# Loads in order of use and residual adds on Pool in a one-layer decoder step

## The reference

```python
h = x + 0.5 * rmsnorm(swiglu(rmsnorm(x, g1pre)), g1post)       # width 2816
b_a, c_a, h_a, u, v = split(rmsnorm(h) @ w_in)                 # 5 x 512 columns
y_a = b_a * causal_dwconv3(c_a * h_a)
y_b = u * (tril(W_s[head]) @ rmsnorm(v) + b_s)                 # chunks of 128 positions
h = h + rmsnorm(concat(rmsnorm(y_a), rmsnorm(y_b)) @ w_out)
h = h + 0.5 * rmsnorm(swiglu(rmsnorm(h)))
h = h + rmsnorm(sigmoid(h @ W_pg) * (p @ W_pp))                # input embedding
```

## Time and profile before

| | us |
|---|---|
| median of three runs | 1377.72 (1377.32 to 1531.78) |
| the profiled execution | 1379.56 |
| its slowest core, first to last instruction (core 7) | 1378.5 |
| its fastest core | 1363.9 |
| TensorE busy on core 7 | 1305.4 |
| Vector, Act, Pool busy | 524.1, 415.0, 94.3 |

### The profile page before, as it was taken

One profiled execution on the slowest core, in us unless ns is written; L12 is line 12 of the kernel. 1 busy time (PEld: TensorE's weight loads), 2 busy tenths in 40 slices (PEclk: granted clock), 3 DMA queues, 4 the chain that ended last, 5 costly groups with the idle time before them and its releaser, 6 DMA issues.

```text
span 1378.5 us, 18493 instructions; the slowest of 8 cores (1363.9 to 1378.5 us)
## 1 busy us (share of the span) xinstructions
PE 1305.4 (95%) x6710; PEld 647.0 (47%) x6710; DVE 524.1 (38%) x691; ACT 415.0 (30%) x860; POOL 94.3 (7%) x185
## 2 busy tenths in 40 slices
PE   5999999999989999999996999999999899999995
PEld 3566664455445666644441444444444344444442
DVE  2322223356677222213365322223466922221337
ACT  3311112344355111111175111123333721111136
POOL 2100000001000200000010000000010020000000
PEclk8999999999999999999997999999999999999998
DMA  9997422129525963231289974321295297423123
GB/s 215 178 222 154 68 47 46 31 45 183 92 42 82 175 124 62 47 69 25 45 202 211 220 159 87 63 53 31 62 175 107 50 147 141 91 48 68 31 39 122
DMA packets 88185, 139.87 MB, mean 101 GB/s; under 512 B 58272, under 2 KB 58528, under 8 KB 87456
## 3 DMA queue, kind: packets, MB, share of 16 engines
q0 software_dynamic: 25296, 90.25, 39.7%
q1 hardware_dynamic: 62800, 48.43, 13.2%
HBM read 206.03 MB, written 9.51 MB: 156 GB/s over the span
## 4 chain that ended last, share of the span: by engine, by line
PE 84%; DVE 6%; DMA 3%; issue 3%; ACT 3%; POOL 0%; DVEq 0%; ACTq 0%; POOLq 0%; SPq 0%
PE ps L218 56%; PE ps L538 23%; PE ps L527 3%; DMA y<-big 2%; DVE zsc L227 2%; DVE nT L227 1%; DVE big L231 1%; DMA h<-xT 1%; ACT big L223 1%; DVE big L227 1%; DMA ring<-w 1%; ACT nT L223 1%; ACT sg L223 1%; ACT L223 1%; DVE nbr L227 1%
## 5 line engine op out<-in xcount | busy, mean ns | idle before, releaser
L218 PE MATMUL ps<-nT,ring 128*128 128x384 bf16 (+1 forms) x4160 | 785.3, 351 | 18.7 <-DVE nT L227 9.2
L218 PEld LDWEIGHTS ps<-nT,ring 128*128 128x128 bf16 x4160 | 409.7, 99 | 392.3 <-issue 44.0
L231 DVE TENSOR_TENSOR big<-ps,sg 128x384 bf16<-128x384 f32 (+1 forms) x220 | 133.9, 610 | 489.4 <-PE ps L218 479.4
L538 PE MATMUL ps<-ring,big 128*128 128x512 bf16 x1320 | 285.5, 379 | 4.5 <-DVE big L231 4.5
L223 ACT ACTIVATE sg<-ps 128x384 f32<-128x384 f32 (+1 forms) x237 | 127.1, 537 | 506.4 <-PE ps L218 496.8
L538 PEld LDWEIGHTS ps<-ring,big 128*128 128x128 bf16 x1320 | 128.9, 98 | 161.0 <-issue 6.2
L259 POOL DMA_DIRECT2D ring<-w x170 | 89.9, 535 | 1104.5 <-PE ps L218 621.6
L223 ACT ACTIVATE big<-ps 128x1024 bf16<-128x1024 f32 (+4 forms) x88 | 75.4, 870 | 229.4 <-PE ps L538 192.4
L227 DVE SCALAR_TENSOR_TENSOR zsc<-ps,st,gains 128x1024 f32<-128x1024 f32 x51 | 65.4, 1282 | 192.5 <-ACT st L223 192.2
L538 PE MATMUL ps<-ring,nT 128*128 128x512 bf16 x480 | 105.4, 379 | 1.0 <-DVE big L231 1.0
L231 DVE TENSOR_TENSOR big<-ps,big 128x384 f32<-128x384 f32 (+3 forms) x77 | 50.8, 686 | 62.1 <-PE ps L218 34.4
(11 more groups left out here) (63 smaller groups left out, 369.3 us busy)
## 6 DMA issues: line engine op xcount, KB each, us to landing
ring<-w POOLq DMA_DIRECT2D x170, 512.0 KB, 14.5
h<-x SPq DMA_DIRECT2D x17, 512.0 KB, 30.7
y<-big SPq DMA_DIRECT2D x13, 512.0 KB, 10.7
gains<-gain SPq DMA_DIRECT2D x12, 512.0 KB, 9.3
h<-xT SPq DMA_DIRECT2D x3, 1536.0 KB, 13.2
big<-xT SPq DMA_DIRECT2D x2, 2048.0 KB, 20.0
y<-zsc SPq DMA_DIRECT2D x4, 512.0 KB, 12.0
big<-pT POOLq DMA_DIRECT2D x2, 512.0 KB, 7.9
```

Of the source, the lines that this page charges most:

```text
L218: ins = nc.tensor.matmul(out_ap, l, r, start=(i == 0), stop=(i == n - 1))
L231: return DVE.mark(nc.vector.tensor_tensor(out=out, in0=in0, in1=in1, op=op))
L538: ins = nc.tensor.matmul(o.t, lhs(k), sv, start=(k == 0), stop=(k == nk - 1))
```

## The change

- Pass 0's tile 1 of x is issued right behind tile 0 and the gain columns; two fills are issued ahead of Pool's last memset, tile 2 of x behind it, then the other fills. Warm-up is 110 matmuls, and 40 more after the statistics of tiles 0 and 1, which now both come ahead of the first stage, as do their applies. Tile 2's squares move to a hook of their own after (1,0), its statistics and apply to the middle of (1,1).
- Pass 1: tile 0 of x is issued by a hook in the down stage when block 8's matmuls are done (the junk output of that stage moves from j0 14 to 0); its squares go to another place in big, over which tile 1's load comes after the statistics. Squares after block 1, statistics after the first group, apply after block 3. Tile 1 of x is issued after the first group; fills at the stage's start are one, and one more after each of two groups. Tile 1's squares and the rest get two hooks.
- Mixer: six square buffers in place of four; `norm_tile` is split, its statistics stay, its apply goes behind the spatial epilogue; group A's statistics go behind U's second projection.
- Output projection and embedding stage: the residual adds are `nc.gpsimd.tensor_tensor` (but for the last block of `ple`). Down stages keep Vector.
- Pass 1, last group of `ple`: the embedding matmuls come ahead of the gate projections, over four pairs.

```diff
...
-    def get_pair():
-        i = rot["pair"] % 3
+    def get_pair(n=3):
+        i = rot["pair"] % n
...
+    def tt_p(wait, out, in0, in1, op):
+        POOL.wait(wait)
+        return POOL.mark(nc.gpsimd.tensor_tensor(out=out, in0=in0, in1=in1, op=op))
...
     xt_load(PASSES[0], 0)
     ev_gc = gc_sem.add(nc.sync.dma_start(out=gc_t[:], in_=gcol_d))
+    xt_load(PASSES[0], 1)
...
+    for _ in range(2):
+        issue_next()
     ev_pc = pchain(nc.gpsimd.memset(carry_t[:], 0.0))
+    xt_load(PASSES[0], 2, [ev_pc])
     while wr["issued"] < NSLOT:
         issue_next()
-    for ti in range(1, 3):
-        xt_load(PASSES[0], ti, [fill_ev[ti - 1][0]])
 
     act([ev_ones], out=st_t[:, 0, 0:1], in_=ones_t[:, 0:1], func=AF.Ln)
-    warm = banks[7]
-    PE.wait(ev_ones)
-    for _ in range(90):
-        ins = nc.tensor.matmul(warm.t[:, 0:128], ones_t[:], ones_t[:], start=True, stop=True)
-    warm.free = PE.mark(ins)
+
+    def warm_up(n):
+        PE.wait(ev_ones, banks[7].free)
+        for _ in range(n):
+            ins = nc.tensor.matmul(banks[7].t[:, 0:128], ones_t[:], ones_t[:], start=True, stop=True)
+        banks[7].free = PE.mark(ins)
+
+    warm_up(110)
...
+    def x_sq_at(P, ti):
+        c0, w = P.tiles[ti]
+        if (P.idx, ti) == (1, 0):
+            return bigf[:, 4096:6144].bitcast(BF16).rearrange("p (k s) -> p k s", k=8)
+        return nT_t[:, :, c0:c0 + w]
...
         for k in range(8):
             PE.wait(sq[k // 2])
-            ins = nc.tensor.matmul(bank.t[:, 0:w], ones_t[:], nT_t[:, k, c0:c0 + w], start=(k == 0), stop=(k == 7))
-        ev = PE.mark(ins)
+            ins = nc.tensor.matmul(bank.t[:, 0:w], ones_t[:], sqt[:, k, :], start=(k == 0), stop=(k == 7))
+        ev = xstat_ev[P.idx, ti] = PE.mark(ins)
...
         e = stt([e3, gain_ev[gi], zfree[zi]], zsc_t[:, zi, :], pt[:], r, gain(gi))
         lo.free = hi.free = e
-        h_ev[b] = zfree[zi] = tt([e], h_t[:, b, :], h_t[:, b, :], zsc_t[:, zi, :], ALU.add)
+        h_ev[b] = zfree[zi] = add([e, h_ev[b]], h_t[:, b, :], h_t[:, b, :], zsc_t[:, zi, :], ALU.add)
...
             last = b == P.nb - 1
             pair, ev = proj_block(P, b, nk, lambda k, b=b: lhs(b, k), 4, fl, wait(b), last)
             if hooks and b in hooks:
-                hooks[b]()
+                hooks[b](ev)
             st = post_stat(b, pair, ev, c, j0)
-            e = post_apply(b, pair, st, gpost)
+            e = post_apply(b, pair, st, gpost, tt if lag == 1 else tt_p)
...
-        sq = [bigf[:, ZR + 2048 + 256 * i:ZR + 2304 + 256 * i].bitcast(BF16) for i in range(4)]
+        sq = [bigf[:, o:o + 256].bitcast(BF16) for o in [ZR + 2048 + 256 * i for i in range(4)] + [ZR + 4096, ZR + 4352]]
...
-        def norm_tile(ti, bank_of=get_bank):
+        def norm_stat(ti, bank_of=get_bank):
+            c0, w = P.tiles[ti]
+            par = ti % 2
+            return rstd_bc(*stat(y_ev[ti][1], w, bank_of), zsc_t[:, par, 512:1024], w, rs_free[par])
...
+        def norm_apply(ti, e_b):
             c0, w = P.tiles[ti]
             par = ti % 2
             ra, rb = zsc_t[:, par, 0:512], zsc_t[:, par, 512:1024]
-            ya, yb, ev_u = y_ev[ti]
-            e_b = rstd_bc(*stat(yb, w, bank_of), rb, w, rs_free[par])
+            ya, _, ev_u = y_ev[ti]
             e = None
             for c in range(8):
...
             if ti >= 1:
-                norm_tile(ti - 1)
+                e_b = norm_stat(ti - 1)
...
-            e_a = rstd_bc(*stat(sqa, w), zsc_t[:, ti % 2, 0:512], w, rs_free[ti % 2])
+            if ti >= 1:
+                norm_apply(ti - 1, e_b)
             sqb = []
             for c in range(4):
                 b, evl = proj(fU, evU, ti, c)
+                if c == 1:
+                    e_a = rstd_bc(*stat(sqa, w), zsc_t[:, ti % 2, 0:512], w, rs_free[ti % 2])
                 y = mixo[:, c, c0:c0 + w]
                 e = tt([evl, mix_e], y, b.t[:, 0:w], y, ALU.mult)
                 b.free = e
@@ -807,8 +832,8 @@
             y_ev[ti] = (e_a, sqb, evl)
         release(fU, evl)
 
-        def tail():
-            norm_tile(nt - 1, get_tp)
+        def tail(ev):
+            norm_apply(nt - 1, norm_stat(nt - 1, get_tp))
...
         if N is not None:
-            xt_load(N, 0, [nT_ev[P.nb - 1]])
-            xt_load(N, 1)
-            pay_owed([nT_ev[P.nb - 1]], NFILL + 3)
+            pay_owed([nT_ev[P.nb - 1]], NFILL + 1)
...
         for gi, grp in enumerate(groups):
             lastg = gi == len(groups) - 1
             sig = {}
+            emb = {}
+            early = N is None and lastg
+            if early:
+                emb = {b: embed(b, b == grp[-1], 4) for b in grp}
             for b in grp:
                 pair, ev = proj_block(P, b, 8, lambda k, b=b: nT_t[:, k, b * 128:(b + 1) * 128], 4, fg, [nT_ev[b]],
-                                      lastg and b == grp[-1])
+                                      lastg and b == grp[-1], 4 if early else 3)
                 gate_ev[b] = ev
-                if N is not None and gi == 2 and b == grp[0]:
-                    xs["st"] = x_stat(N, 0, xs["sq"], get_tp)
                 pt, lo, hi = pair
                 e = act([ev, gb_guard(b)], out=gb(b), in_=pt[:], func=AF.Sigmoid)
                 lo.free = hi.free = e
                 sig[b] = e
+                if N is not None and b == 1:
+                    xs["sq"] = x_square(N, 0)
+                if N is not None and b == 3:
+                    x_apply(N, 0, *xs["st"], [gate_ev[3]])
                 del nT_ev[b]
             zev = {}
             for b in grp:
-                pair = get_pair()
+                pair, ev = emb[b] if early else embed(b, lastg and b == grp[-1])
...
-                xs["sq"] = x_square(N, 0, [gate_ev[3]])
             st = {}
             for b in grp:
                 st[b] = rstd_of(gb(b), sg_t[:].rearrange("p a s -> p (a s)"), [zev[b]], D)
-            if N is not None and gi == 2:
-                xs["ev"] = x_apply(N, 0, *xs["st"])
+            if N is not None and gi == 0:
+                xs["st"] = x_stat(N, 0, xs["sq"], get_tp)
             for b in grp:
                 r, e3 = st[b]
                 e = stt([e3, gain_ev[base + GPLE]], gb(b), gb(b), r, gain(base + GPLE))
                 nxt["stt"] = e
-                e = tt([e], gb(b), gb(b), h_t[:, b, :], ALU.add)
+                e = (tt if b == P.nb - 1 else tt_p)([e], gb(b), gb(b), h_t[:, b, :], ALU.add)
                 SP.wait(e)
                 out_ev[b] = y_sem[b].add(nc.sync.dma_start(out=y_d[P.rows[b]:P.rows[b] + 128, :], in_=gb(b)))
                 if N is not None and b < N.nb:
                     h_free[b] = e
+            if N is not None and not lastg:
+                pay_owed(None, NFILL + 2 + gi)
+                if gi == 0:
+                    xt_load(N, 1, [xstat_ev[1, 0]])
...
-    x_apply(PASSES[0], 0, *x_stat(PASSES[0], 0, x_square(PASSES[0], 0), get_bank))
-
-    def start_mid(ti):
-        def f():
-            x_apply(PASSES[0], ti, *x_stat(PASSES[0], ti, x_square(PASSES[0], ti), get_bank))
-        return f
+    first = x_stat(PASSES[0], 0, x_square(PASSES[0], 0), get_bank)
+    x_apply(PASSES[0], 0, *first)
+    second = x_stat(PASSES[0], 1, x_square(PASSES[0], 1), get_bank)
+    warm_up(40)
+    x_apply(PASSES[0], 1, *second)
...
+    def start_square():
+        nx["sq"] = x_square(PASSES[0], 2)
+
+    def start_mid():
+        x_apply(PASSES[0], 2, *x_stat(PASSES[0], 2, nx["sq"], get_bank))
...
+    def next_square():
+        nx["sq"] = x_square(PASSES[1], 1)
+
     def next_mid():
-        e = x_apply(PASSES[1], 1, *x_stat(PASSES[1], 1, x_square(PASSES[1], 1), get_bank))
+        e = x_apply(PASSES[1], 1, *x_stat(PASSES[1], 1, nx["sq"], get_bank))
         SP.wait(e)
         for b in range(PASSES[1].nb):
             x_load(PASSES[1], b, [h_free[b]])
...
         if P.idx == 0:
-            gu_stage(P, 2, guard1, {(0, 0): (0, start_mid(1)), (1, 0): (1, start_mid(2)), (2, 0): (0, start_loads),
+            gu_stage(P, 2, guard1, {(1, 0): (1, start_square), (1, 1): (0, start_mid), (2, 0): (0, start_loads),
                                     (8, 0): (0, late_consts)},
                      [(0, 0), (0, 1), (1, 0), (1, 1), (0, 2), (1, 2)])
         else:
-            gu_stage(P, 3, guard1, {(0, 0): (1, next_mid)})
+            gu_stage(P, 3, guard1, {(0, 0): (1, next_square), (1, 0): (1, next_mid)})
...
         hold_fills(1)
 
+        def next_x(ev):
+            xt_load(PASSES[1], 0, [ev])
...
         tok_stage(P, NFF, 6, lambda b, k: hmid[:, k, b * 128:(b + 1) * 128], lambda b: [hm["ev"]],
-                  base + G2POST, 4.0, 1, 14, cast)
+                  base + G2POST, 4.0, 1, 0, cast, {8: next_x} if N is not None else None)
...
```

More of the change, by code:

```diff
@@ L463, in build_program @@
     xn_ev = {}
+    xstat_ev = {}
+    def x_sq_at(P, ti):
[3 more added lines that the diff above has]
+        return nT_t[:, :, c0:c0 + w]
     def x_square(P, ti, wait=None):
         c0, w = P.tiles[ti]
+        sqt = x_sq_at(P, ti)
```

(64 more changed lines are left out.)

## The result

The changed kernel takes 1366.04 us in the median, 0.9912 of the kernel before, interval [0.9884, 0.9941]: 12 us gained where 35 were forecast. The profiled execution took 1364.25, its slowest core (core 3) 1363.2, against 1378.5 before.

The account below looks back on a forecast made before the run. TensorE was taken as the bound, with time to win only where it waits or runs at its lower clock. Gains 6 + 11 + 0 + 17 + 1 = 35 us against the median 1377.72 gave 1343, range 1326 to 1365.

Parts of the forecast that it names:

- Start: Start of the first pass: x tile 1 loaded earlier lands at 19, first stage ends at 201.6 against 208.25; 6 us gained.
- Mixer: Mixer tiles: moved statistics and norm save 16.9 us, less 5.8 for new waits; 11 us gained, bounds 7 and 16.
- Output projections: Residual adds moved to Pool in the output projections: 3.6 us per block, no change; bounds 5 gained, 7 lost.
- the formula (4.9 + A)/2 = 3.6: Output projections: time per block of a four-engine loop over two blocks, A being Pool's add, taken as 2.3 us.
- The rival: Pool's add and Vector's two-SBUF-input instructions exclude each other: output projections lose 10.5 us, embedding stage 4; 1358 in all; chance 0.3.
- Embedding: First pass's embedding stage and the stage behind it: earlier x load and reordering gain 17 us, bounds 8 and 22.
- the rival of loads bound by the DMA: Transfers slow one another, whatever their order: start gains 2 us, embedding 8; 1356 in all; chance 0.15.
- End: Last group of the second pass's embedding stage, embedding matmuls first: 1 us gained, between 0 and 2.

## Why the prediction was wrong

**Start: right.** Tile 1's squares began at 18.52 (said: 19), the first weight matmul at 24.63 (25.7), and the down stage at 203.05 (201.6). The wait for tile 2's apply came where said, in single matmuls behind single applies: from 24.63 to 51.25 TensorE had 135 matmuls and 8 of statistics, 23.3 us, and took 26.6, so 3.3 us against 2.8.

**Mixer: right.** The two stages gained 13.1, but the first block of the output projection, which waited 4.29 (said: 3.4), then ran at a granted clock of 0.67: 5.30 us for 16 matmuls instead of 3.61. With these 1.7 us the gain is 11.4, said 11, and 9.5 by the kernel with this part undone. The term had the wait and not the clock behind it; the order with the last tile's norm behind its U products takes both away.

**Output projections: the step that failed.** The length of Pool's add was right, 2.35 for an assumed 2.3. What failed was the formula (4.9 + A)/2 = 3.6, a loop in which each engine's instruction keeps its own length. Its terms were lengths measured with Pool idle, and the sum was set at no change although three operations with two SBUF inputs were to run side by side, with nothing in the trace that said they could. Eight intervals of 0.64 make 5.1, the clock 1.7, together the 6.8 of pass 0; pass 1 lost 3.3. Not all of it is the lock: 6.0 us are by the kernel with the input in PSUM, and 2.2 stay without it, in the first two intervals of each pass, of which the formula knows nothing (its steady part was near: 3.72 a block there, 3.63 by the formula with A = 2.35); another 2.2 came behind the blocks, by the lower clock. The rival named the mechanism, the place and the price (4.3 apart, 10.5 us; measured 4.24 in pass 0, 3.99 in pass 1, and 9.9 in the kernel before with only the adds moved), and was given 0.3. The row's 10.1 agrees with its 10.5 partly by luck: it holds the mixer's 1.7 and not the 2.2 behind. The Trainium skill (SBUF — State Buffer, Who interferes with whom) states an exclusive lock on a shared pair of ports between the two engines. The traces agree in what they can show: each engine waits for the other's end (3.27 for 2.35, 3.25 for 1.28), and neither does where one input of Vector's lies in PSUM; that it is a pair of ports no run shows. The rival's own last part, 4 us in the embedding stage, did not come: slowed scaled embeddings cost nothing measurable there.

The lock alone doesn't make 1366. Against the 35 us of the sum the stages fell short by 10.1 here, 7.4 in the embedding, 0.8 + 1.3 at start and end, 2.2 in the gate/up stages behind the output projections, and brought 2.1 more in the mixers: 19.7, which is 35 - 15.3.

**Embedding: mechanism half right, size wrong.** Said: 17; it was 9.6 on the slowest cores, 5 by the kernel with this part undone. Four things. The load of x took 10.5 us and its squares came at 692.38, so that they stood in front of block 2's sigmoid at their worst place: TensorE waited 3.57, not 1.7. Behind this wait the granted clock was 0.62 (below), and eight statistics' matmuls took 3.46 instead of 1.89. The next stage's first matmul waited 2.19 for a product. And the stage behind waited for the stores of blocks 6 to 8 longer than said, since the owed fills go out beside them (six halves from 738.86 on, within 4 us): 5 us by the two kernels that differ in this alone. The forecast took the stores' lateness for a matter of their position, and did not ask which fills go out beside them. The rival of loads bound by the DMA was right in this part: fills slow the stores. Whether they slow x is open: tile 0 took 14.7 us before the change, with the second load and six halves of fills right behind it, and 8.4 to 10.5 by core after it, with no fill out before it had landed; no kernel separates the two. And core 7's loss was no good measure of the term: core 0 took 12 us less for the same two stages.

**End.** Between 0 and 2 was said; 49.0 became 49.3; why is open.

## What to carry to other kernels

Moving an operation to another engine is priced by what runs beside it, not by its own length: before a two-input SBUF operation goes to Pool, look at which of Vector's instructions with two SBUF inputs will meet it, and if one of them lies in the loop that frees PSUM, leave it on Vector or give one of the inputs a place in PSUM. A wait that an in-order engine causes moves to the next thing in its queue: moving the squares, then the scaling, gave back in the next stage what it gained, and the embedding stage's time came with the fills alone. Fills that nobody needs yet belong behind the stores whose buffers somebody waits for.

## What the runs showed of the hardware

- Pool's add of 128x1024 fp32 with both inputs in SBUF takes 2.35 us alone; beside a Vector instruction with two SBUF inputs one of the two waits for the other's end (2.35 and 1.28 became 3.27 and 3.25 us). Beside a Vector instruction with one input in PSUM both keep their length.
- After 3.57 us of waiting TensorE's granted clock was 0.62 for the next 4.3 us, after 4.29 us of it 0.67 for 5.2 us: for most of both stretches the lower of its levels, 1.2 and not 2.4 GHz. These waits cost about 1.5 and 1.7 us more than their length: the next 12 matmuls took 4.12 us and the next 16 took 5.14 by their starts, where 0.216 each would be 2.59 and 3.46. The table of stretches of the changed kernel (stretch: length, busy us and instructions of PE, PEld, DVE, ACT, POOL, then granted clock, DMA share, GB/s) ahead of and behind the first wait, and right behind the second and after it:

```profile
691.80:697.30 5.50, 1.95 (x10) 0.69 (x8) 2.35 (x2) 4.92 (x6) 1.05 (x2) 1.00 0.57 143
697.30:701.60 4.30, 4.28 (x13) 1.72 (x14) 2.51 (x2) 3.94 (x9) 0.00 (x0) 0.62 1.05 200
...
380.80:386.00 5.20, 5.20 (x17) 2.06 (x18) 2.15 (x4) 1.08 (x3) 0.00 (x0) 0.67 0.00 0
386.50:404.00 17.50, 17.50 (x82) 7.75 (x80) 11.67 (x10) 11.64 (x31) 7.01 (x3) 1.00 0.08 16
```

- The last store of the embedding stage, 512 KB, landed after 10.5 to 13.3 us by core where the owed fills went out beside it, and after 3.8 to 8.8 us where they followed it.
